# PEER layer on one Trainium2 core: the gelu-times-gate product moved between engines, and scores issued one query visit earlier

## The chip, the cores and the metric

The kernel runs on one core of a Trainium2 chip. The metric is the device time of one execution in microseconds; the lower the better. Three runs of the kernel before gave 4600.65, 4601.71 and 4601.87 us.

## What is computed

One layer of an encoder, in float32, for 1024 prompt tokens and 256 sample tokens of width 1024, with shared weights: two attentions, gated and merged, and then the expert retrieval that this change is about, followed by a norm:

```python
def peer(h, w_query, sub_keys, expert_u, expert_v):      # per chunk of 128 tokens
    qry = einsum('cd,dq->cq', xc, w_query).reshape(128, 8, 2, 128)
    sc = einsum('chpd,hpnd->chpn', qry, sub_keys)          # 8 heads, 2 halves, 128 keys
    s_top, i_top = top_k(sc, 16)
    cand = s_top[:, :, 0, :, None] + s_top[:, :, 1, None, :]
    best_s, pos = top_k(cand, 16)                          # 16 of 128*128 experts a head
    g = softmax(best_s)
    act = gelu(einsum('chkd,cd->chk', expert_u[idx], xc))
    return einsum('chk,chkd->cd', g * act, expert_v[idx])
```

So each token has 128 chosen experts, each with a gate g. The weight of an expert is g times gelu of a dot product.

## The kernel before, in words

The attentions and the whole sample part come first and are the same in both kernels. The change lies in the last phase, `phase_mixed` (L1663), over the eight tiles of 128 prompt tokens. Five of them (0 to 4, GATHERED) gather the rows of their experts; for three (5 to 7, DENSE) all 16384 experts are computed and multiplied by a dense table of gates.

**Order.** Every engine has its own program. All of them are written by the same walk, `Turns.walk` (L1571), which calls named pieces of work in one order; each engine does its share of a piece and skips those in which it has none. An engine does its work strictly in that order and waits on semaphores for the others.

**Queries.** The first loop of the walk has 39 visits v (L1574). Visit v issues query v (32 of them: TensorE, 16 matmuls, L2270) and, on ScalarE, the copy of query v-1 (L1949). Two queries make the 2 x 128 key scores of a head for four tiles. At odd visits from 3 on TensorE computes the scores (L2284); at the visit behind that ScalarE copies them out of PSUM (L1959) and stores them to DRAM, from where SP loads them, one head of one tile at a time (L1802). From visit 6 on VectorE picks (`choose`, L2090): the top 16 of each half, of the candidates, and decodes them to indices; the gates are made by `soften` and `gates` (L2143).

**Steps.** A step (n, g) works on pair g of the 128 chosen experts of gathered tile n; there are 64 + 1 for each tile. GpSimd gathers the rows u and v of an expert for 128 tokens in one indirect DMA (L1921) into a ring of 8 slots, that is 4 pairs, and may overwrite a pair when TensorE has `used` it. In step (n, g):
- VectorE (L2174) waits for gelu of pair g-1, multiplies ge by the gates g2 of that pair (L2178), and then computes the two dot products of pair g (L2186).
- ScalarE (L2009) waits for the dots of pair g and applies gelu to them (L2013); then it waits for the weights of pair g-1 and spreads each over a small diagonal matrix (L2020, two instructions).
- TensorE (L2309) waits for the diagonals of pair g-1 and multiplies the v rows by them (L2320, 32 small matmuls).

So everything of pair g-1 behind the gelu is done one step later than its dots. Steps are put between other work by `advance` (L1534): from visit 13 on one or two at a visit, by `1 + v % 2`, then among the building of the dense gates, then in the dense stage in proportion to planned costs (L1653).

**Dense tiles.** After the picks, VectorE, ScalarE and TensorE build one-hot matrices and the gates (L2170, L1993, L1995, L2305); ScalarE copies them (L2002) and stores them to DRAM, 2 MB at a time, from two buffers (L2006). Then the dense stage: 128 stage1 units (L2340, gelu on ScalarE at L2044) and 192 stage2 units (L2356, added on VectorE at L2221), with the other 237 steps between them.

Of the kernel before, what the change touches and what calls it, by code (L numbers as in the profile page):

```python
# [9 lines left out]
ALU = mybir.AluOpType  # L10
# [21 lines left out]
HEADS, KEYS, TOPK = 8, 128, 16  # L32
# [1492 lines left out]
class Turns:  # L1525
# [45 lines left out]
    def walk(self):  # L1571
        on, first, every = self.on, DENSE[0], slice(0, HEADS)
        ends = {0: 0, 1: 1, 3: 2, 5: 4, 7: 6}
        for v in range(39):  # L1574
            if v < 32:
# [3 lines left out]
            if v == 1:  # L1579
                on("late")  # L1580
            if v % 2 and 3 <= v <= 33:
                on("scores", (v - 3) // 2)
            if v % 2 == 0 and 4 <= v <= 34:
                on("spread_s", (v - 4) // 2)
            h, at = divmod(v - 6, 4)
            if 0 <= h < HEADS and at == 0:
# [8 lines left out]
            if h >= 0 and at == 3 and h < HEADS:  # L1595
                self.pick_dense(first + 1, h)
            if v >= 13:
                self.advance(1 + v % 2)
# [64 lines left out]
def phase_mixed(nc, tag, x2, g_ffn, w_query, sub_keys, experts, u_turned, g_final, ident_d, iota_d, fold_d, unfold_d,  # L1663
# [7 lines left out]
    with ExitStack() as ctx:  # L1671
# [65 lines left out]
        h_ld, row_ld = [m.sem(f"h_ld{b}") for b in range(2)], [m.sem(f"row_ld{r}") for r in range(RING)]  # L1737
        dotted, gelued, weighted, diag_ready, used = (m.sem(n) for n in ("dotted", "gelued", "weighted", "diag_ready", "used"))
        xr_ld, parts_ready, unfolded, y_ready, root2 = (m.sem(n) for n in ("xr_ld", "parts_ready", "unfolded", "y_ready", "root2"))
# [10 lines left out]
        order = []  # L1750
        Turns(lambda what, *a: order.append(a[:2]) if what == "choose" and a[2] == 0 else None).walk()

        def walk(**do):
# [33 lines left out]
        with nc.Block() as block:  # L1787
# [138 lines left out]
            def _(act):  # L1926
# [82 lines left out]
                def step(n, g):  # L2009
                    if g < STEPS:  # L2010
                        act.wait_ge(dotted, SLOTS * n + PAIR * (g + 1))
                        c = slice(PAIR * g, PAIR * (g + 1))
                        nc.scalar.activation(ge[:, c], dot[:, c], ACT.Gelu).then_inc(gelued, 1)  # L2013
                    if g >= 1:
                        act.wait_ge(weighted, STEPS * n + g)
                        if STEPS * n + g > 2:
                            act.wait_ge(used, STEPS * n + g - 2)
                        for c in range(PAIR):
                            s = PAIR * (g - 1) + c
                            last = nc.scalar.activation(diag[:, (g - 1) % 2, c, :], fold[:], ACT.Copy, scale=wgt[:, s:s + 1])  # L2020
                        last.then_inc(diag_ready, 1)
                    if n and g == 2:
                        norm_y(n)
# [41 lines left out]
            def _(dve):  # L2065
# [77 lines left out]
                def gates(tile, hs):  # L2143
                    nonlocal gated
                    gated += 1
                    to = gd_of(tile - DENSE[0]) if tile in DENSE else g2[:, tile % 2, :]
                    dve.wait_ge(exp_ready, gated)
                    link(nc.vector.reduce_sum(ssum[:, hs], soft_of(tile)[:, hs, :], AXX))
                    link(nc.vector.reciprocal(ssum[:, hs], ssum[:, hs]))
                    link(nc.vector.tensor_tensor(to.rearrange("p (h c) -> p h c", c=TOPK)[:, hs, :], soft_of(tile)[:, hs, :],  # L2150
                                                 ssum[:, hs].unsqueeze(2).to_broadcast([P, hs.stop - hs.start, TOPK]), ALU.mult))

                def turn(d):
# [20 lines left out]
                def step(n, g):  # L2174
                    if g >= 1:
                        dve.wait_ge(gelued, STEPS * n + g)
                        c = slice(PAIR * (g - 1), PAIR * g)
                        nc.vector.tensor_tensor(wgt[:, c], ge[:, c], g2[:, n % 2, c], ALU.mult).then_inc(weighted, 1)  # L2178
                    if g == 0 and n:
# [310 lines left out]
```

## Time and profile before

| | us |
|---|---|
| median of 3 runs | 4601.71 |
| the profiled execution | 4601.26 |
| its span, from first to last instruction | 4599.5 |
| the last phase starts its queries at | 2098 |
| first VectorE pick | 2138.4 |
| first unit of the dense stage that runs without a hole | 2901 |

The profile is of one execution. Engines: PE is TensorE, PEld its weight loads, DVE VectorE, ACT ScalarE, POOL GpSimd, SP the queue of SyncE. An L number is a line of the kernel.

### The profile page before, as it was taken

The page shows a single profiled execution, that of the slowest core. Times are in us where ns is not written, and L with a number is a line of the kernel's source. Part 1 is how long each engine was busy: PE and PEld are TensorE (multiplying, and loading weights), DVE is VectorE, ACT ScalarE, POOL GpSimd, SP SyncE. Part 2 cuts the span into 40 slices and gives each one's busy share as a digit, 9 for nine tenths or more (in the row PEclk, how much of TensorE's full clock was granted, in tenths as well). Part 3 has the DMA queues.
Part 4 walks back from the last instruction along what each step waited for, and adds up shares of the span by engine and source line. Part 5 has one row for each costly group of instructions (what it writes and reads, how often), then busy time and mean ns, then how long its engine had stood idle before and what let it go on. Part 6 is the DMA issues. An engine that isn't in the chain of part 4 may idle for free.

```text
span 4599.5 us, 61350 instructions
## 1 busy us (share of the span) xinstructions
PE 3988.8 (87%) x22629; PEld 2057.9 (45%) x22629; DVE 2836.5 (62%) x7114; ACT 1128.4 (25%) x2916; POOL 1254.2 (27%) x1018
## 2 busy tenths in 40 slices
PE   7786599998799989998983456799999999999998
PEld 3454444443577764444441334344444444444443
DVE  1332856775888876662778977455565556555544
ACT  0221111221455551112222565111111111111111
POOL 0200232221534513320232212233323323332332
PEclk9888799999899999998995688899999999999999
DMA  6243398896544348756688779999999999999997
GB/s 238 76 179 120 109 364 318 336 356 230 209 175 178 147 171 337 300 222 233 256 318 318 285 276 369 360 401 380 387 388 405 382 379 412 406 398 377 408 413 303
DMA packets 351290, 1370.42 MB, mean 298 GB/s; under 512 B 26896, under 2 KB 112528, under 8 KB 231568
## 3 DMA queue, kind: packets, MB, share of 16 engines
q0 software_dynamic: 129024, 939.58, 51.6%
q1 hardware_dynamic: 161840, 389.17, 22.6%
q10 hardware_dynamic: 60128, 37.75, 2.6%
q8 instruction: 180, 2.95, 0.3%
q14 instruction: 118, 0.97, 0.1%
HBM read 1277.22 MB, written 89.18 MB: 297 GB/s over the span
## 4 chain that ended last, share of the span: by engine, by line
PE 34%; DVE 10%; DMA 6%; issue 3%; ACT 2%; POOL 0%; SPq 0%; DVEq 0%; ACTq 0%; another core or an unknown queue 0%
PE prompt_exp_wk L2340 13%; PE prompt_exp_wk L2356 11%; PE prompt_exp_acc L2320 6%; DVE prompt_exp_junk L2186 4%; PE prompt_exp_wk L2270 4%; DMA prompt_exp_ring<-in_experts_dram,prompt_exp_idx 3%; DMA gates_dram<-prompt_exp_area 2%; DVE prompt_exp_hT L2170 1%; DVE prompt_exp_hit L2130 1%; DVE prompt_exp_topi L2081 1%; ACT prompt_exp_diag L2020 1%; PE prompt_exp_wk L2305 1%; DVE prompt_exp_top L2078 0%; DMA scores_dram<-prompt_exp_area 0%; PE prompt_exp_wk L2284 0%
## 5 line engine op out<-in xcount | busy, mean ns | idle before, releaser
L1921 POOL DMA_INDIRECT prompt_exp_ring<-in_experts_dram,prompt_exp_idx x640 | 698.6, 1092 | 1815.9 <-PE prompt_exp_acc L2320 1603.4
L2186 DVE CUSTOM_DVE_ANT_0 prompt_exp_junk<-prompt_exp_ring,prompt_exp_h 128x1024 bf16<-128x1024 f32 x640 | 765.2, 1223 | 167.6 <-DMA prompt_exp_ring<-in_experts_dram,prompt_exp_idx 166.9
L2340 PE MATMUL prompt_exp_wk<-prompt_exp_hT,prompt_exp_area 128*128 128x384 f32 x2048 | 697.5, 495 | 23.7 <-DMA prompt_exp_area<-in_u_turned_dram 23.7
L2356 PE MATMUL prompt_exp_wk<-prompt_exp_area 128*128 128x512 f32 x1536 | 702.8, 604 | 0.0
L537 PE MATMUL prompt_proj_acc<-normed_w,normed_hT 128*128 128x512 f32 x1280 | 553.7, 595 | 14.5 <-PEq L91 14.5
L2340 PEld LDWEIGHTS prompt_exp_wk<-prompt_exp_hT,prompt_exp_area 128*128 128x128 f32 x2048 | 385.8, 192 | 357.9 <-issue 97.6
L2320 PE MATMUL prompt_exp_acc<-prompt_exp_ring,prompt_exp_diag 32*32 32x512 f32 x10240 | 392.9, 643 | 173.5 <-ACT prompt_exp_diag L2020 170.3
L152 POOL DMA_INDIRECT sample_hid_ring<-in_experts_dram,sample_hid_idx x256 | 277.0, 1082 | 892.1 <-DVE sample_hid_acc L182 842.8
L2221 DVE TENSOR_TENSOR prompt_exp_area<-prompt_exp_area,prompt_exp_wk 128x512 f32<-128x512 f32 x186 | 127.8, 687 | 575.9 <-PE prompt_exp_wk L2356 543.4
L2356 PEld LDWEIGHTS prompt_exp_wk<-prompt_exp_area 128*128 128x128 f32 x1536 | 280.4, 190 | 425.8 <-issue 395.3
L537 PEld LDWEIGHTS prompt_proj_acc<-normed_w,normed_hT 128*128 128x128 f32 x1280 | 243.6, 191 | 318.4 <-issue 318.4
L165 DVE CUSTOM_DVE_ANT_0 sample_hid_junk<-sample_hid_ring,sample_hid_h 128x1024 bf16<-128x1024 f32 x256 | 349.9, 1367 | 44.2 <-DMA sample_hid_ring<-in_experts_dram,sample_hid_idx 33.8
L2013 ACT ACTIVATE prompt_exp_ge<-prompt_exp_dot 128x2 f32<-128x2 f32 x320 | 64.9, 203 | 1272.1 <-DVE prompt_exp_dot L2186 1265.8
L182 DVE SCALAR_TENSOR_TENSOR sample_hid_acc<-sample_hid_ring,sample_hid_w,sample_hid_acc 128x1024 f32<-128x1024 f32 x254 | 326.2, 1284 | 7.5
L2320 PEld LDWEIGHTS prompt_exp_acc<-prompt_exp_ring,prompt_exp_diag 32*32 32x32 f32 x10240 | 79.6, 106 | 375.9 <-ACT prompt_exp_diag L2020 253.4
L2305 PE MATMUL prompt_exp_wk<-prompt_exp_area,prompt_exp_hT 128*128 128x128 f32 x768 | 132.7, 342 | 112.9 <-DVE prompt_exp_hT L2170 76.4
L2305 PEld LDWEIGHTS prompt_exp_wk<-prompt_exp_area,prompt_exp_hT 128*128 128x128 f32 x768 | 122.3, 250 | 157.8 <-DVE prompt_exp_hT L2170 102.3
L2020 ACT ACTIVATE prompt_exp_diag<-prompt_exp_fold,prompt_exp_wgt 128x32 f32<-128x32 f32 x640 | 165.8, 306 | 11.6 <-DVE prompt_exp_wgt L2178 11.4
L2044 ACT ACTIVATE prompt_exp_area<-prompt_exp_wk 128x384 f32<-128x384 f32 x128 | 62.8, 490 | 358.4 <-PE prompt_exp_wk L2340 358.1
L537 PE MATMUL sample_proj_acc<-sample_proj_w,sample_proj_hT 128*128 128x512 f32 x320 | 140.5, 601 | 9.4 <-PEq L271 9.4
L998 PE MATMUL prompt_att_Op<-prompt_att_vB,prompt_att_pT_b 128*128 128x128 f32 x1024 | 125.9, 276 | 10.4 <-ACT prompt_att_pT_a L712 10.4
L174 DVE TENSOR_TENSOR sample_hid_w<-sample_hid_ge,sample_hid_g 128x1 f32<-128x1 f32 (+1 forms) x208 | 59.1, 284 | 115.0 <-ACT sample_hid_ge L203 114.8
(363 smaller groups left out, 5025.4 us busy)
## 6 DMA issues: line engine op xcount, KB each, us to landing
prompt_exp_area<-in_u_turned_dram SPq DMA_DIRECT2D x128, 512.0 KB
prompt_exp_area<-in_experts_dram SPq DMA_DIRECT2D x64, 1024.0 KB
gates_dram<-prompt_exp_area ACTq DMA_DIRECT2D x12, 2048.0 KB
prompt_exp_area<-gates_dram SPq DMA_DIRECT2D x32, 768.0 KB
sample_proj_w<-in_w_all_dram SPq DMA_DIRECT2D x10, 2048.0 KB, 20.0
normed_w<-in_w_all_dram SPq DMA_DIRECT2D x10, 2048.0 KB, 13.7
proj_dram<-prompt_proj_stage SPq DMA_DIRECT2D x80, 256.0 KB
prompt_exp_ring<-in_experts_dram,prompt_exp_idx POOLq DMA_INDIRECT x640
```

The costliest lines, as they stand in the source:

```text
L152: self.nc.gpsimd.indirect_dma_start(out=self.ring[:, s % self.RING, :], out_offset=None, in_=self.experts, in_offset=bass.IndirectOffsetOn ...
L165: self.nc.vector.tensor_tensor_reduce(out=self.junk[:], in0=self.ring[:, s % self.RING, 0:D], in1=self.h[:], scale=1.0, scalar=0.0, op0=AL ...
L182: nc.vector.scalar_tensor_tensor(self.acc[:], v, w, self.acc[:], ALU.mult, ALU.add).then_inc(self.added, 1)
L537: last = nc.tensor.matmul(acc[:, u % 4, :], hT[:, k, t * P:(t + 1) * P], w[:, c % NL, k, :], start=(k == 0), stop=(k == KD - 1))
L1921: nc.gpsimd.indirect_dma_start(out=ring[:, s % RING, :], out_offset=None, in_=experts, in_offset=bass.IndirectOffsetOnAxis(ap=idx[:, n % 2 ...
L2020: last = nc.scalar.activation(diag[:, (g - 1) % 2, c, :], fold[:], ACT.Copy, scale=wgt[:, s:s + 1])
L2186: nc.vector.tensor_tensor_reduce(out=junk[:, s % 2, :], in0=ring[:, s % RING, 0:D], in1=h2[:, n % 2, :], scale=1.0, scalar=0.0, op0=ALU.mu ...
L2270: last = nc.tensor.matmul(wk[:, v % 2, :], wq[:, h // 2 % 2, k, at:at + P], (hT1 if grp else hT0)[:, k, :], start=(k == 0), stop=(k == KD ...
L2305: last = nc.tensor.matmul(wk[:, 2 + i % 2, c * KEYS:(c + 1) * KEYS], onehot_a[:, i % 2 * BLOCK + c, :], onehot_b[:, i % 2, c, :], start=Tr ...
L2320: last = nc.tensor.matmul(acc[at:at + Q, part, :], diag[k, (g - 1) % 2, c, :], ring[k, s % RING, D + half * 512:D + half * 512 + 512], sta ...
L2340: last = nc.tensor.matmul(wk[:, j % 2, 0:TURNED], ut[:, j % 3, k, :], hT_dense[:, k, :], start=(k == 0), stop=(k == KD - 1))
L2356: last = nc.tensor.matmul(wk[:, 2 + o % 2, :], act_e[:, c % 2, j, t * P:(t + 1) * P], vt[:, half, j, :], start=(j == 0), stop=(j == JB - 1))
```

## The change

Two things. First, the loop of visits has 38 instead of 39; scores are computed at even visits from 2 on, in the order of the walk right behind the query of that visit, and all that follows them (copies and stores of scores, picks, gates, the steps from visit 12) moves one visit earlier. Second, the product of gelu and gate leaves VectorE: ScalarE makes it in its own part of the step, one instruction of one column for each of the two experts of the pair (a copy with the gate as its scale), between gelu of pair g and the diagonals of pair g-1. ScalarE waits for the gates by a new semaphore, once for each head, and for gelu of the pair; VectorE no longer waits for gelu, and before it writes gates over those of two tiles back it waits for that tile's last diagonals.

```diff
--- before.py
+++ after.py
@@ -1571,18 +1571,18 @@
     def walk(self):
         on, first, every = self.on, DENSE[0], slice(0, HEADS)
         ends = {0: 0, 1: 1, 3: 2, 5: 4, 7: 6}
-        for v in range(39):
+        for v in range(38):
             if v < 32:
                 on("query", v)
             if 1 <= v <= 32:
                 on("spread_q", v - 1)
             if v == 1:
                 on("late")
+            if v % 2 == 0 and 2 <= v <= 32:
+                on("scores", (v - 2) // 2)
             if v % 2 and 3 <= v <= 33:
-                on("scores", (v - 3) // 2)
-            if v % 2 == 0 and 4 <= v <= 34:
-                on("spread_s", (v - 4) // 2)
-            h, at = divmod(v - 6, 4)
+                on("spread_s", (v - 3) // 2)
+            h, at = divmod(v - 5, 4)
             if 0 <= h < HEADS and at == 0:
                 self.pick(GATHERED[0], h)
                 if h in ends:
@@ -1594,7 +1594,7 @@
                 self.pick_dense(first, h)
             if h >= 0 and at == 3 and h < HEADS:
                 self.pick_dense(first + 1, h)
-            if v >= 13:
+            if v >= 12:
                 self.advance(1 + v % 2)
         done = 0
 
@@ -1735,7 +1735,7 @@
         ij_ready, ij_turned, ij_spread = (m.sem(n) for n in ("ij_ready", "ij_turned", "ij_spread"))
         a_ready, b_ready, gp_full, gp_spread = (m.sem(n) for n in ("a_ready", "b_ready", "gp_full", "gp_spread"))
         h_ld, row_ld = [m.sem(f"h_ld{b}") for b in range(2)], [m.sem(f"row_ld{r}") for r in range(RING)]
-        dotted, gelued, weighted, diag_ready, used = (m.sem(n) for n in ("dotted", "gelued", "weighted", "diag_ready", "used"))
+        gates_ready, dotted, gelued, weighted, diag_ready, used = (m.sem(n) for n in ("gates_ready", "dotted", "gelued", "weighted", "diag_ready", "used"))
         xr_ld, parts_ready, unfolded, y_ready, root2 = (m.sem(n) for n in ("xr_ld", "parts_ready", "unfolded", "y_ready", "root2"))
         yo_ready, out_stored = m.sem("yo_ready"), m.sem("out_stored")
         u_ld, v_ld, gc_ld = [m.sem(f"u_ld{b}") for b in range(3)], [m.sem(f"v_ld{b}") for b in range(2)], [m.sem(f"gc_ld{b}") for b in range(2)]
@@ -1749,6 +1749,12 @@
 
         order = []
         Turns(lambda what, *a: order.append(a[:2]) if what == "choose" and a[2] == 0 else None).walk()
+
+        gate_order = []
+        Turns(lambda what, *a: gate_order.extend([a] if what == "gates" and a[0] in GATHERED else [])).walk()
+
+        def gates_upto(tile, h):
+            return 1 + next(i for i, (t, hs) in enumerate(gate_order) if t == tile and hs.start <= h < hs.stop)
 
         def walk(**do):
             Turns(lambda what, *a: do.get(what, idle)(*a)).walk()
@@ -2012,11 +2018,18 @@
                         c = slice(PAIR * g, PAIR * (g + 1))
                         nc.scalar.activation(ge[:, c], dot[:, c], ACT.Gelu).then_inc(gelued, 1)
                     if g >= 1:
+                        pair = slice(PAIR * (g - 1), PAIR * g)
+                        if pair.start % TOPK == 0:
+                            act.wait_ge(gates_ready, gates_upto(n, pair.start // TOPK))
+                        act.wait_ge(gelued, STEPS * n + g)
+                        for s in range(pair.start, pair.stop):
+                            last = nc.scalar.activation(wgt[:, s:s + 1], ge[:, s:s + 1], ACT.Copy, scale=g2[:, n % 2, s:s + 1])
+                        last.then_inc(weighted, 1)
                         act.wait_ge(weighted, STEPS * n + g)
                         if STEPS * n + g > 2:
                             act.wait_ge(used, STEPS * n + g - 2)
-                        for c in range(PAIR):
-                            s = PAIR * (g - 1) + c
+                        for s in range(pair.start, pair.stop):
+                            c = s % PAIR
                             last = nc.scalar.activation(diag[:, (g - 1) % 2, c, :], fold[:], ACT.Copy, scale=wgt[:, s:s + 1])
                         last.then_inc(diag_ready, 1)
                     if n and g == 2:
@@ -2144,11 +2157,15 @@
                     nonlocal gated
                     gated += 1
                     to = gd_of(tile - DENSE[0]) if tile in DENSE else g2[:, tile % 2, :]
+                    if tile in GATHERED and tile >= 2 and hs.start == 0:
+                        dve.wait_ge(diag_ready, STEPS * (tile - 1))
                     dve.wait_ge(exp_ready, gated)
                     link(nc.vector.reduce_sum(ssum[:, hs], soft_of(tile)[:, hs, :], AXX))
                     link(nc.vector.reciprocal(ssum[:, hs], ssum[:, hs]))
                     link(nc.vector.tensor_tensor(to.rearrange("p (h c) -> p h c", c=TOPK)[:, hs, :], soft_of(tile)[:, hs, :],
                                                  ssum[:, hs].unsqueeze(2).to_broadcast([P, hs.stop - hs.start, TOPK]), ALU.mult))
+                    if tile in GATHERED:
+                        dve.sem_inc(gates_ready, 1)
 
                 def turn(d):
                     dve.sem_inc(ij_ready, 1)
@@ -2172,10 +2189,6 @@
                     last.then_inc(a_ready, 1)
 
                 def step(n, g):
-                    if g >= 1:
-                        dve.wait_ge(gelued, STEPS * n + g)
-                        c = slice(PAIR * (g - 1), PAIR * g)
-                        nc.vector.tensor_tensor(wgt[:, c], ge[:, c], g2[:, n % 2, c], ALU.mult).then_inc(weighted, 1)
                     if g == 0 and n:
                         dve.wait_ge(h_ld[n % 2], 16 * ((n + 1) // 2))
                     if g < STEPS:
```

## Rows read from the trace of the kernel before

**Rows 1.** The profile page: span, and the busy time of each engine.
```profile
span 4599.5 us, 61350 instructions
PE 3988.8 (87%) x22629; PEld 2057.9 (45%) x22629; DVE 2836.5 (62%) x7114; ACT 1128.4 (25%) x2916; POOL 1254.2 (27%) x1018
```

**Rows 2.** Busy time by stage of the last phase: start:end, length, engines, clock, DMA share, GB/s.
```profile
2098.00:2200.00 102.00, 100.56 (x313) 51.29 (x314) 38.33 (x198) 22.16 (x38) 7.49 (x8) 0.99 0.51 194
2200.00:2434.00 234.00, 201.46 (x1480) 90.60 (x1478) 178.75 (x664) 50.83 (x144) 64.48 (x61) 0.92 0.82 313
2434.00:2650.00 216.00, 92.58 (x979) 55.05 (x979) 199.07 (x725) 92.24 (x262) 47.73 (x48) 0.61 0.76 285
2650.00:2855.00 205.00, 116.33 (x1343) 81.20 (x1344) 164.41 (x508) 122.48 (x322) 50.01 (x50) 0.83 0.89 324
2855.00:2901.00 46.00, 20.17 (x153) 10.31 (x152) 13.40 (x46) 5.04 (x17) 7.91 (x7) 0.80 1.01 380
2901.00:4584.00 1683.00, 1631.13 (x11200) 714.88 (x11200) 931.30 (x2196) 244.60 (x875) 520.98 (x468) 0.99 0.98 389
```

**Rows 3.** Chain of waits, in order of time: start, length, what.
```profile
2134.39 13.74 PE prompt_exp_wk L2270 x32
2148.13 1.78 PE prompt_exp_wk L2284 x16
...
2668.61 26.37 DMA gates_dram<-prompt_exp_area
...
3513.60 3.65 PE prompt_exp_wk L2356 x8
```

**Rows 4.** Waits of TensorE, 2901 to 4600: us in total, times, longest.
```profile
PE prompt_exp_acc L2320 <- ACT prompt_exp_diag L2020: 43.8, 49, 6.7
PE prompt_exp_wk L2340 <- DMA prompt_exp_area<-in_u_turned_dram: 23.7, 1, 23.7
```

**Rows 5.** Timeline of one step in the dense stage: start, length, engine, line.
```profile
3517.27 0.69 DVE L2221 TENSOR_TENSOR prompt_exp_area<-prompt_exp_area,prompt_exp_wk 128x512 f32<-128x512 f32 x1 [6.13 <-PE prompt_exp_wk L2356]
...
3517.88 0.15 DVE L2178 TENSOR_TENSOR prompt_exp_wgt<-prompt_exp_ge,prompt_exp_g 128x2 f32<-128x2 f32 x1
3517.95 1.22 DVE L2186 CUSTOM_DVE_ANT_0 prompt_exp_junk<-prompt_exp_ring,prompt_exp_h 128x1024 bf16<-128x1024 f32 x1
...
3520.36 0.20 ACT L2013 ACTIVATE prompt_exp_ge<-prompt_exp_dot 128x2 f32<-128x2 f32 x1 [7.29 <-DVE prompt_exp_dot L2186]
3520.47 0.52 ACT L2020 ACTIVATE prompt_exp_diag<-prompt_exp_fold,prompt_exp_wgt 128x32 f32<-128x32 f32 x2
...
3521.03 1.15 PE L2320 MATMUL prompt_exp_acc<-prompt_exp_ring,prompt_exp_diag 32*32 32x512 f32 x32 [0.37 <-ACT prompt_exp_diag L2020]
```

**Rows 6.** Timeline of the next step, whose diagonals are just in time.
```profile
3526.82 0.52 ACT L2020 ACTIVATE prompt_exp_diag<-prompt_exp_fold,prompt_exp_wgt 128x32 f32<-128x32 f32 x2
3527.48 1.14 PE L2320 MATMUL prompt_exp_acc<-prompt_exp_ring,prompt_exp_diag 32*32 32x512 f32 x32
```

**Rows 7.** ScalarE's square root of one column with an operand from memory: ns min/median/max.
```profile
L1933 ACT ACTIVATE prompt_exp_stat<-prompt_exp_stat,prompt_exp_eps x8: 294/294/297, 2083.1 to 2101.7; 128x1 f32<-128x1 f32 x8
```

**Rows 8.** Timeline, building of the gates: absolute values, relu, blocks.
```profile
2706.04 1.26 ACT L1993 ACTIVATE prompt_exp_area<-prompt_exp_iota,prompt_exp_ijgT 128x128 f32<-128x128 f32 x4
...
2707.33 0.63 ACT L1995 ACTIVATE prompt_exp_area<-prompt_exp_area 128x512 f32<-128x512 f32 x1
...
2708.06 2.02 PE L2305 MATMUL prompt_exp_wk<-prompt_exp_area,prompt_exp_hT 128*128 128x128 f32 x16 [0.72 <-issue]
```

**Rows 9.** Waits in 2200 to 2434 (first) and 2650 to 2855 (the others).
```profile
DVE prompt_exp_wgt L2178 <- ACT prompt_exp_ge L2013: 7.9, 14, 2.8
...
DVE prompt_exp_wgt L2178 <- ACT prompt_exp_ge L2013: 6.0, 3, 4.5
...
PE prompt_exp_acc L2320 <- ACT prompt_exp_diag L2020: 38.8, 19, 8.7
```

**Rows 10.** Timeline: VectorE's first pick of the last phase.
```profile
2138.38 0.49 DVE L2078 MAX8 prompt_exp_top<-prompt_exp_scl 128x8 f32<-128x128 f32 x2 [34.35 <-DMA prompt_exp_scl<-scores_dram]
```

## The prediction

> **What bounds the kernel now.** The page comes first: one core, a span of 4599.5 us in a profiled execution of 4601.26, with TensorE busy 87% and ScalarE 25% [rows 1]. That share says ScalarE has room; it does not say whether anybody waits for it. So the second view is the busy time by stage [rows 2], over the last phase alone, the only one that the change touches. The first 2098 us keep their time. Then come: queries alone (to about 2200), queries with picks and the first steps (to 2434), the tail of the picks (to 2650, VectorE busy 199 of 216 us), the building of the dense gates (to 2855), a hole while the last gates are stored (to 2901), and the dense stage of 1683 us, with TensorE busy 97% of it and the DMA engines 98%.
>
> The third view, the chain of waits, says who sets the end of each [rows 3]. Early it runs through the queries: a pair of them takes 13.7 us, with 1.8 of scores behind it. In the building it runs twice through a store of gates (the first 26 us), with stretches of TensorE, VectorE and ScalarE between. In the dense stage it is TensorE's own matmuls, one behind the other. So in that stage, each time TensorE stands idle is paid in full, and the fourth view lists these: 49 times, 43.8 us together, TensorE waits for the diagonals of ScalarE [rows 4].
>
> **What such a wait is made of** [rows 5]. Two stage2 units stand back to back. VectorE adds the first (3517.27), multiplies the weights of the last pair (3517.88), makes two dot products (3517.95 to 3520.33); ScalarE does gelu (3520.36), then two diagonals (3520.47 to 3520.99); TensorE starts at 3521.03, 0.37 us late. The diagonals belong to the pair before and have all they need, but ScalarE is an in-order engine and takes them behind the gelu that waits for the new dots. Most of the waits have exactly this 0.37; nine are over 1 us, most of them where a gathered row came late. Where a stage1 unit (5.4 us) or another step stands in between, there is slack: of the 237 steps of the stage, read one by one, four of those that don't wait have under 0.5 us (the tightest that one sees 0.10 [rows 6]), some 30 have 0.6 to 1.0 and the rest more.
>
> **Part 1: the product moves to ScalarE.** VectorE loses one instruction per step, 0.155 us long, but the dot behind it starts 0.07 us after it, so 0.07 is what a busy VectorE gains in the dense stage [rows 5]. It loses the wait for gelu as well. ScalarE gains per step two products of 128x1 whose scale is read from memory, and a wait for its own result, ahead of the diagonals. No row shows this product. Nearest is the square root of 128x1 with an operand from memory, 0.294 [rows 7]; two diagonals overlap so that the second starts 0.21 behind the first [rows 5]; an engine that waits for its own result resumes 0.03 behind it [rows 8]. That is 0.21 + 0.29 + 0.03 = 0.53. Bounds: from below two operations as cheap as gelu, which lets the next one start after 0.11 and lasts 0.20 [rows 5]: 0.34; from above two diagonals of 0.31 that don't overlap, with two waits: 0.68. I take 0.5, since the square root is nearest in size and kind and a column fewer than the diagonal's 32 helps the overlap. Less VectorE's 0.07: the diagonals are ready 0.43 later (0.27 to 0.61).
> The Trainium skill speaks against this half (ScalarE: Activation LUTs, Rules for kernel authors): a plain multiplication belongs on VectorE. By that rule alone the half is a loss wherever ScalarE is waited for; without it the sum below would be the 7 us of part 2 and the kernel would come to 4594. The trace agrees as far as it goes: one instruction of 0.155 us does both columns on VectorE, in the rows above.
>
> Dense stage: 49 x 0.43 = **+21 us** (13 to 30). The four tight ones add under 1, and the ones at 0.6 and more are not reached. What the delay hides in: where a row came late TensorE waits 1.2 to 6.7 us, and as rows are requested behind earlier steps, a slower TensorE gives them some of that back: I take **-3** (0 to -10).
>
> Building of the gates: here TensorE waits 19 times for diagonals, 38.8 us [rows 9]. ScalarE is in the loop: behind the diagonals it makes four absolute values and a relu, and TensorE's blocks start 0.10 us after that relu ends [rows 8]; VectorE's next block waits for them. So 0.43 per step goes into the loop, but not where ScalarE then waits for a store anyway. 14 of the 24 steps: **+6** (0 to +10). The 6.0 us that VectorE waits for gelu [rows 9] give nothing: 4.5 of them come while ScalarE sits behind a store of gates, and its diagonals come no sooner.
>
> Where VectorE is the bound (some 30 steps between 2254 and 2650): 0.1 us each for the instruction, and part of the 7.9 us of waits for gelu before 2434 [rows 9], which fall between the two steps of an odd visit: **-4** (-1 to -10).
>
> The new waits: for the gates of a tile, and of the gates for the diagonals of two tiles back. Both are satisfied long before. The first is signalled by VectorE ahead of the dots for which ScalarE has just waited; the second comes at step 55 of the tile before, over 50 steps after the diagonals it asks for. The third, for gelu, is of the operation one step back. Queued behind them are gelu of the dense units and the blocks, priced above. Nothing is cast for them: cover gone, they would cost a step.
>
> **Part 2: scores one visit earlier.** Scores, their copies, stores and loads (ScalarE's and SP's queues), picks, gates and steps all keep their places to each other; only the queries move one visit back. VectorE's first pick waits 34.35 us for scores [rows 10], behind four queries; now behind three, so 6.9 us sooner. PE, the copies and the banks allow it: the second query's copy ends during the third query. The steps start one query sooner and the tail has one visit fewer; the number of steps before the dense stage stays 39 + 49. Whether queries or VectorE set the pace in between, one query's time is gone: **-7 us** (0, if late scores or rows fill the gap, to -10, a visit's length once steps run in it).
>
> **Sum.** -7 - 4 + 6 + 21 - 3 = +13. On the profiled 4601.3 this gives **4614 us**; the median of the runs, 4601.7, is 0.4 more and changes nothing.
>
> **Rivals.**
> (a) The dense stage is paced by DMA, not TensorE: its engines are 98% taken at 389 GB/s [rows 2]. Then the added waits vanish in the rows' landing and the sum is -7 - 4 + 6 = -5: 4596, no change. For it: the share. Against: TensorE's idle time in the stage comes from the diagonals, and of its waits for data only one, at the start, is for a DMA of weights [rows 4]. 0.22.
> (b) Faster: VectorE, freed of its wait for gelu, runs ahead where it is the bound. It takes hold if over half of the 14 waits before 2434 and of the slots there lie on the chain, and the building's stores swallow ScalarE's part: -10 - 10 + 0, and the dense stage gives at most +5 through (a): 4586. For it: VectorE's 199 of 216 us. Against: in the dense stage TensorE's waits were seen. 0.15.
> (c) ScalarE's products don't overlap: 0.61 net, 49 x 0.61 = 30, building +10, no relief: 4629. 0.10.
> (d) The scores part brings nothing, as VectorE finds its scores or rows late after all: 4621. 0.08.
> My forecast (4605 to 4622) has 0.45.
>
> **The numbers.** A measurement of this kernel can tell 0.2%, 9.2 us, from no change: under 4592.5 is faster, over 4610.9 slower. Faster: (b) and an edge of (a), 0.18. Same: the rest of (a), and the forecast's lower edge, where the product is as cheap as its lower bound, 0.31. Slower 0.51. The range from 4590 to 4628 leaves out most of (b) and half of (c). The forecast's own is 4605 to 4622.
>
> **What would show it.** The new products near 0.29 us, the diagonals starting some 0.6 us behind gelu in place of 0.11. In the dense stage the typical wait goes from 0.37 to 0.8, and TensorE's waits for diagonals from 43.8 us to about 65; the stage from 1683 to about 1700. VectorE's first pick 6.9 us earlier, at 2131.5; the dense stage starting within 5 us of before. I am wrong if the waits grow and the stage doesn't (a), if the start of the dense stage comes 15 us or more sooner (b), or if the product costs under 0.2.

## The result, and the profile after

Over 20 runs of each, before has a median of 4601.48 us and the changed kernel one of 4612.24: a ratio of 1.0022, 95% interval 1.0016 to 1.0029. That is 10.8 us slower by the medians: clear of no change, and about the 0.2% that a measurement here can tell. Two executions of before took 6192.01 and 14898.58 us; they are left out of the ratio. The profiled execution of the changed kernel took 4617.22, 5 us above its median, while that of before (4601.26) stands at its median.

The page's head, against [rows 1]: ScalarE has 640 instructions and 151 us more, VectorE 320 instructions and 36 us less, TensorE the same number of matmuls.

```profile
span 4615.4 us, 61687 instructions
...
PE 3997.3 (87%) x22629; PEld 2063.3 (45%) x22629; DVE 2800.2 (61%) x6794; ACT 1279.5 (28%) x3556; POOL 1241.1 (27%) x1018
```

The same stages as [rows 2], each cut where the changed kernel reaches the same point (start:end, length, PE, PEld, DVE, ACT, POOL, clock, DMA share, GB/s):

```profile
2098.00:2200.00 102.00, 100.58 (x314) 51.01 (x313) 46.55 (x240) 22.28 (x37) 7.51 (x8) 0.99 0.51 191
2200.00:2434.00 234.00, 201.39 (x1510) 89.51 (x1508) 177.15 (x626) 67.73 (x214) 67.14 (x64) 0.92 0.86 330
2434.00:2638.00 204.00, 91.79 (x979) 55.75 (x979) 186.25 (x671) 101.71 (x303) 42.98 (x44) 0.60 0.76 281
2638.00:2850.00 212.00, 128.65 (x1345) 90.27 (x1314) 162.13 (x479) 132.72 (x367) 55.13 (x49) 0.77 0.88 317
2850.00:2895.66 45.66, 19.84 (x151) 10.05 (x149) 12.19 (x41) 6.79 (x25) 6.78 (x8) 0.74 0.97 370
2895.66:4615.40 1719.74, 1633.98 (x11216) 714.27 (x11216) 916.00 (x1970) 364.11 (x1362) 506.49 (x468) 0.99 0.97 382
```

The last line counts the stage to its end; before it is

```profile
2901.06:4599.50 1698.44, 1634.31 (x11216) 715.39 (x11216) 940.55 (x2207) 252.64 (x888) 520.98 (x468) 0.99 0.97 387
```

So TensorE is busy for the same 1634 us in a stage that is 21.3 us longer: all of the difference is idle time. The wait that carries it, in place of the 43.8 us of [rows 4] (columns as there):

```profile
PE prompt_exp_acc L2333 <- ACT prompt_exp_diag L2033: 65.1, 54, 6.6
```

and one such wait, the same step as in [rows 5]:

```profile
3516.48 0.69 DVE L2234 TENSOR_TENSOR prompt_exp_area<-prompt_exp_area,prompt_exp_wk 128x512 f32<-128x512 f32 x1 [6.05 <-PE prompt_exp_wk L2369]
...
3517.08 1.22 DVE L2199 CUSTOM_DVE_ANT_0 prompt_exp_junk<-prompt_exp_ring,prompt_exp_h 128x1024 bf16<-128x1024 f32 x1
...
3519.49 0.20 ACT L2019 ACTIVATE prompt_exp_ge<-prompt_exp_dot 128x2 f32<-128x2 f32 x1 [7.51 <-DVE prompt_exp_dot L2199]
3519.60 0.47 ACT L2026 ACTIVATE prompt_exp_wgt<-prompt_exp_ge,prompt_exp_g 128x1 f32<-128x1 f32 x2
3520.10 0.53 ACT L2033 ACTIVATE prompt_exp_diag<-prompt_exp_fold,prompt_exp_wgt 128x32 f32<-128x32 f32 x2
...
3520.68 1.15 PE L2333 MATMUL prompt_exp_acc<-prompt_exp_ring,prompt_exp_diag 32*32 32x512 f32 x32 [0.81 <-ACT prompt_exp_diag L2033]
```

VectorE's add to the first dot is 0.60 us where it was 0.68. Gelu to the first diagonal is 0.61 where it was 0.11. The wait is 0.81 where it was 0.37: 0.44 more. The product by itself (ns least/median/most), the square root's 0.294 of [rows 7] beside it:

```profile
L2026 ACT ACTIVATE prompt_exp_wgt<-prompt_exp_ge,prompt_exp_g x640: 277/279/297, 2205.7 to 4588.7; 128x1 f32<-128x1 f32 x160
```

The first pick, against [rows 10]:

```profile
2130.79 0.49 DVE L2091 MAX8 prompt_exp_top<-prompt_exp_scl 128x8 f32<-128x128 f32 x2 [28.07 <-DMA prompt_exp_scl<-scores_dram]
```

Its place relative to the first query, 34.2 us in place of 40.4, is the fairer reading, since the phase starts 1.4 us sooner in this execution. Cut into three lengths, queries and picks / building to the start of the dense stage / dense stage: before 399.6 / 403.5 / 1698.4 us, after 389.0 / 410.0 / 1719.7. (Building starts where ScalarE first copies the turned picks, at 2497.6 and 2485.6.) The dense stage thus starts 5.4 us sooner than in before.

Each such length is of one execution. Two kernels were profiled twice (e3 and e10, e7 and e11 below), and their lengths differ by 2.2 and 3.0 us in the first stretch, 0.2 and 0.7 in the second, 2.4 and 0.6 in the third. Differences of that size say nothing here. The spans of before and after differ by 15.9 us, the medians by 10.8.

### The profile page after: what moved, and what is told of

It reads as the page before. It is cut to its first block, busy times and chain, and to the rows that moved or that the text cites. A ratio compares the mean times of both kernels' runs of the same rounds, so it can differ in the third digit from the quotient of the medians.

```text
span 4615.4 us, 61687 instructions
## 1 busy us (share of the span) xinstructions
PE 3997.3 (87%) x22629; PEld 2063.3 (45%) x22629; DVE 2800.2 (61%) x6794; ACT 1279.5 (28%) x3556; POOL 1241.1 (27%) x1018
## 3 DMA queue, kind: packets, MB, share of 16 engines
q8 instruction: 180, 2.95, 0.3%
## 4 chain that ended last, share of the span: by engine, by line
PE 32%; DVE 10%; DMA 7%; issue 3%; ACT 2%; POOL 1%; SPq 0%; DVEq 0%; ACTq 0%; POOLq 0%
PE prompt_exp_wk L2353 12%; PE prompt_exp_wk L2369 10%; PE prompt_exp_acc L2333 6%; DMA prompt_exp_ring<-in_experts_dram,prompt_exp_idx 4%; DVE prompt_exp_junk L2199 4%; PE prompt_exp_wk L2283 3%; DMA gates_dram<-prompt_exp_area 2%; DVE prompt_exp_hT L2187 1%; PE prompt_exp_wk L2318 1%; DVE prompt_exp_topi L2094 1%; DVE prompt_exp_hit L2143 1%; ACT prompt_exp_diag L2033 1%; POOL prompt_exp_ring L1927 1%; ACT prompt_exp_wgt L2026 1%; DVE prompt_exp_top L2091 0%
## 5 line engine op out<-in xcount | busy, mean ns | idle before, releaser
L1927 POOL DMA_INDIRECT prompt_exp_ring<-in_experts_dram,prompt_exp_idx x640 | 686.0, 1072 | 1844.9 <-PE prompt_exp_acc L2333 1641.2
L2318 PE MATMUL prompt_exp_wk<-prompt_exp_area,prompt_exp_hT 128*128 128x128 f32 x768 | 142.9, 361 | 103.5 <-DVE prompt_exp_hT L2187 76.8
L2318 PEld LDWEIGHTS prompt_exp_wk<-prompt_exp_area,prompt_exp_hT 128*128 128x128 f32 x768 | 132.0, 267 | 149.5 <-DVE prompt_exp_hT L2187 112.9
L2026 ACT ACTIVATE prompt_exp_wgt<-prompt_exp_ge,prompt_exp_g 128x1 f32<-128x1 f32 x640 | 148.9, 280 | 0.0
## 6 DMA issues: line engine op xcount, KB each, us to landing
prompt_exp_area<-gates_dram SPq DMA_DIRECT2D x32, 768.0 KB, 13.5
```

Of the source, the lines that this page charges most:

```text
L1927: nc.gpsimd.indirect_dma_start(out=ring[:, s % RING, :], out_offset=None, in_=experts, in_offset=bass.IndirectOffsetOnAxis(ap=idx[:, n % 2 ...
L2026: last = nc.scalar.activation(wgt[:, s:s + 1], ge[:, s:s + 1], ACT.Copy, scale=g2[:, n % 2, s:s + 1])
L2318: last = nc.tensor.matmul(wk[:, 2 + i % 2, c * KEYS:(c + 1) * KEYS], onehot_a[:, i % 2 * BLOCK + c, :], onehot_b[:, i % 2, c, :], start=Tr ...
```

## The experiments

Eleven kernels, in three groups that each shared their runs of before: e1 to e4 (4599.36 us), e5 to e8 (4601.93) and e9 to e11 (4599.11). Ratios are to before of the same group.

### The two halves apart

e1 is the changed kernel with the old walk, so the product alone; e2 is before with the new walk, so the scores alone.

```diff
 # e1, in the changed kernel
-        for v in range(38):
+        for v in range(39):
...
-            if v % 2 == 0 and 2 <= v <= 32:
-                on("scores", (v - 2) // 2)
+            if v % 2 and 3 <= v <= 33:
+                on("scores", (v - 3) // 2)
 # e2: the same lines the other way round, in the kernel before
```

> The change's first half alone: product on ScalarE, scores at their old visits. Theory (ScalarE's two products lie on TensorE's path in the dense stage, and the two halves add): 4612 plus the 7 us of the second half, so 4619 us (4615 to 4624), 1.0035 to 1.005 of the kernel before; TensorE's waits for the diagonals in the dense stage about 65 us, as in the changed kernel; VectorE's first pick at 2138. Rival (the scores part brings nothing): 4612, no slower than the changed kernel.

> The change's second half alone: scores one visit earlier, product on VectorE. Theory: 7 us less than before, 4594 us (4590 to 4598), waits for the diagonals in the dense stage about 44 us as before, building of the gates starting about 8 us sooner. Rival (the earlier scores are hidden by late rows, and the 12 us by which the building starts sooner come from the product): 4601, building starting at its old time.

e1: 4622.09 us, 1.0052 (1.0038 to 1.0065). e2: 4587.45, 0.9969 (0.9956 to 0.9981). Both are clear of no change, on opposite sides: +22.7 and -11.9 us. Added they give the +10.8 that was measured. Scores alone gave more than expected. TensorE's waits in the dense stage follow the product and not the scores (e1, then e2):

```profile
PE prompt_exp_acc L2333 <- ACT prompt_exp_diag L2033: 64.6, 54, 6.6
```

```profile
PE prompt_exp_acc L2320 <- ACT prompt_exp_diag L2020: 45.4, 51, 6.7
```

By stage, e1 has 400.7 / 405.0 / 1719.1 and e2 385.8 / 404.3 / 1701.1 us. So the product costs 1.1, 1.5 and 20.7 us against before, and 3.2, 5.7 and 18.6 as the changed kernel against e2. The scores bring 13.8 us (e2 against before) and 11.7 (the changed kernel against e1) in the queries and picks; the later stretches are 3.5 and 5.6 us longer and give part of it back.

### Is it the product, or where it stands?

In each step ScalarE first waits for the new dots (gelu of pair g), then makes product and diagonals of pair g-1, which had all they need. e3 keeps all of the change and only puts the waiting part last. e4 does the same to the kernel before.

```diff
-                    if g < STEPS:
-                        act.wait_ge(dotted, SLOTS * n + PAIR * (g + 1))
-                        c = slice(PAIR * g, PAIR * (g + 1))
-                        nc.scalar.activation(ge[:, c], dot[:, c], ACT.Gelu).then_inc(gelued, 1)
                     if g >= 1:
...
                         last.then_inc(diag_ready, 1)
+                    if g < STEPS:
+                        act.wait_ge(dotted, SLOTS * n + PAIR * (g + 1))
+                        c = slice(PAIR * g, PAIR * (g + 1))
+                        nc.scalar.activation(ge[:, c], dot[:, c], ACT.Gelu).then_inc(gelued, 1)
```

> The changed kernel with ScalarE's order in a step turned round: products and diagonals of the pair before, which have all they need, and only then gelu, which waits for the new dots. Theory (the price is paid because the diagonals stand behind that gelu): waits of TensorE for diagonals in the dense stage fall from 65 us to under 27, the stage gets some 35 us shorter, and the time is about 4573 us (4566 to 4582). Rival (DMA paces the dense stage): the waits turn into waits for rows, and the time stays over 4595.

> The kernel before with the same order in ScalarE's step: diagonals before gelu, product still on VectorE at the head of its step. Theory: the dense stage's waits fall from 44 us to under 27, the building's by some us, the time by 20 to 25 us to about 4579 (4572 to 4587). Rival (DMA paces the stage): over 4595. If the product on ScalarE is harmless once it is off the path, this one is slower than the third of this call by the 7 us of the scores, and no more than that.

e3: 4530.19 us, 0.9849 (0.9835 to 0.9862). e4: 4549.1, 0.9893 (0.9878 to 0.9908). Both beat their expectation by far (4573 and 4579 were written down). TensorE's waits in the dense stage, e3 and then e4:

```profile
PE prompt_exp_acc L2333 <- ACT prompt_exp_diag L2029: 8.8, 3, 6.4
```

```profile
PE prompt_exp_acc L2320 <- ACT prompt_exp_diag L2016: 14.3, 5, 4.7
```

The typical short wait is gone, not shortened. In e3's timeline the diagonals don't wait for the next dots: they are ready at 3400.5, ScalarE then waits 5.24 us for dots, and TensorE uses them at 3405.97 without any wait:

```profile
3399.98 0.53 ACT L2029 ACTIVATE prompt_exp_diag<-prompt_exp_fold,prompt_exp_wgt 128x32 f32<-128x32 f32 x2
...
3405.75 0.20 ACT L2034 ACTIVATE prompt_exp_ge<-prompt_exp_dot 128x2 f32<-128x2 f32 x1 [5.24 <-DVE prompt_exp_dot L2199]
...
3405.97 1.14 PE L2333 MATMUL prompt_exp_acc<-prompt_exp_ring,prompt_exp_diag 32*32 32x512 f32 x32
```

More came than the 43.8 us of waits could explain, and the windows say from where (dense stage of e3, then of e4; columns as above):

```profile
2877.35:4528.80 1651.45, 1622.33 (x11216) 711.42 (x11216) 921.66 (x1970) 374.30 (x1362) 514.31 (x468) 0.99 0.99 398
```

```profile
2886.21:4545.00 1658.79, 1622.98 (x11216) 712.45 (x11216) 943.80 (x2207) 268.63 (x888) 528.10 (x468) 0.99 0.98 396
```

e4's stage is 39.6 us shorter than that of before. Of this, 29.5 is the wait for diagonals (43.8 to 14.3) and 11.3 is TensorE's own busy time (1634.31 to 1622.98), for the same number of matmuls. Ahead of the stage, queries and picks take 388.8 us in e4 and 371.6 in e3; building (404.8 and 407.5) gained nothing.

### Each microsecond in that place

e5 doubles the products: it makes each of them a second time, into a column that nobody reads.

```diff
-                        for s in range(pair.start, pair.stop):
-                            last = nc.scalar.activation(wgt[:, s:s + 1], ge[:, s:s + 1], ACT.Copy, scale=g2[:, n % 2, s:s + 1])
+                        for to, s in [(to, s) for to in (stat, wgt) for s in range(pair.start, pair.stop)]:
+                            last = nc.scalar.activation(to[:, s:s + 1] if to is wgt else stat[:, 0, 8 + s % PAIR:9 + s % PAIR],
+                                                        ge[:, s:s + 1], ACT.Copy, scale=g2[:, n % 2, s:s + 1])
```

> The changed kernel with each product made twice on ScalarE (the first pair goes to columns that nobody reads), so four products ahead of the diagonals. The trace of the changed kernel shows two products in 0.47 us, 0.19 apart, so this adds 0.38 us to each step. Theory: the dense stage's 54 waits grow by 0.38 each, some 20 us, and steps that had 0.1 to 0.4 us of slack join them: waits for diagonals from 65 to about 90 us, time 4612 + 25 = 4637 us (4630 to 4650). Rival (the 21 us of the dense stage come from VectorE's changed timing or from DMA, not from the length of ScalarE's work): within 5 us of 4612.

4629.81 us, 1.006 (1.0046 to 1.0074): slower than the changed kernel again, by 17.6 us, where 4637 was written down.

```profile
PE prompt_exp_acc L2333 <- ACT prompt_exp_diag L2033: 79.2, 53, 6.6
```

```profile
3529.91 1.15 PE L2333 MATMUL prompt_exp_acc<-prompt_exp_ring,prompt_exp_diag 32*32 32x512 f32 x32 [1.19 <-ACT prompt_exp_diag L2033]
```

The typical wait goes 0.37, 0.81, 1.19: by 0.4 with each pair of products. Sorted by size, the waits of up to 1.25 us are 42 of 17.6 us in before, 45 of 36.2 in the changed kernel and 45 of 49.4 here. So the typical wait grows by what stands ahead of it, each time, but the sum of the short ones by 18.6 and then by 13.2 us only. The longer waits stay about as they are (7 of 26.2 us, 9 of 28.9, 8 of 29.8). The dense stage is 7.8 us longer than in the changed kernel: 14.1 us more of waits, but 5.5 us less of busy time (the last section says where that comes from).

### Where in time, and which part must come first

e6 makes the product on ScalarE only up to the end of the building of the gates (step 16 of the second tile), and on VectorE, ahead of the dots, from then on. e7 is e2 with the order of e3: scores moved, product on VectorE, gelu last. e8 is the changed kernel with its two products alone ahead of the wait for the dots, while the diagonals stay behind gelu.

```diff
 # e6, VectorE's step
+                    if g >= 1 and late_pair(n, g):
+                        dve.wait_ge(gelued, STEPS * n + g)
...
+                        nc.vector.tensor_tensor(wgt[:, c], ge[:, c], g2[:, n % 2, c], ALU.mult).then_inc(late_weighted, 1)
 # e8, ScalarE's step: the products move up
+                    if g >= 1:
+                        act.wait_ge(gelued, STEPS * n + g)
...
+                        last.then_inc(weighted, 1)
                     if g < STEPS:
                         act.wait_ge(dotted, SLOTS * n + PAIR * (g + 1))
```

> The changed kernel with the product back on VectorE from step (1, 17) on, which is where the dense stage begins; before it ScalarE makes it. Theory: the dense stage is as long as before (1698 to 1701 us, waits for diagonals 44 us), what lies ahead of it is as in the changed kernel; time 4612 - 20 = 4591 us (4585 to 4597). If the product costs as much ahead of the dense stage as the two half changes suggest (their dense stages start at 2884 and 2896), it stays some 4 us above the kernel with the scores part alone, else level with it.

> Scores one visit earlier, product on VectorE, diagonals before gelu on ScalarE. It differs from the fastest so far (4530 us) only in who makes the product. Theory (with the diagonals first, neither gelu nor ScalarE's products are waited for by TensorE, and VectorE is nearer to being the bound): 4536 us (4530 to 4545), the product on ScalarE being worth 0 to 10 us. Rival (a plain product is dearer on ScalarE in any order): under 4528.

> The changed kernel with only the two products moved ahead of gelu in ScalarE's step; the diagonals stay behind gelu. ScalarE does exactly as much. Theory (what costs is the products' place, not their presence): the diagonals again start 0.11 us behind gelu, waits in the dense stage 41 to 46 us, time 4588 us less what VectorE gains, 4585 (4578 to 4592). Rival (any more work on ScalarE costs this): 4607 to 4617.

e6: 4590.46 us, 0.9976 (0.9967 to 0.9985). e7: 4539.39, 0.9859 (0.9842 to 0.9876). e8: 4583.85, 0.9958 (0.9944 to 0.9973).

e6 against e2 (0.9969, in another group; the intervals overlap): having ScalarE multiply while VectorE is the bound brings nothing that can be seen (queries and picks 385.6 us against e2's 385.8). In the building it costs 7.0 us (411.3 against 404.3). Its 45.5 us of waits in the dense stage are e2's 45.4. e8 says that the product costs nothing once nobody stands behind it. Its products and e2's are the same work on two engines, and e8 is not slower:

```profile
PE prompt_exp_acc L2334 <- ACT prompt_exp_diag L2034: 40.5, 48, 6.6
```

```profile
3515.67 0.20 ACT L2027 ACTIVATE prompt_exp_ge<-prompt_exp_dot 128x2 f32<-128x2 f32 x1 [6.86 <-DVE prompt_exp_dot L2200]
3515.78 0.52 ACT L2034 ACTIVATE prompt_exp_diag<-prompt_exp_fold,prompt_exp_wgt 128x32 f32<-128x32 f32 x2
...
3516.35 1.15 PE L2334 MATMUL prompt_exp_acc<-prompt_exp_ring,prompt_exp_diag 32*32 32x512 f32 x32 [0.29 <-ACT prompt_exp_diag L2034]
```

Gelu to diagonal is 0.11 again, and the wait 0.29 in place of before's 0.37, since VectorE has one instruction fewer ahead of its dots. That is the 0.08 for which the prediction took 0.07.

### With the order right, which engine should multiply?

e9 is e1 with gelu last (product on ScalarE, scores as before). e10 is e3 over again, e11 is e7 over again, all in one group.

```diff
 # e9 = e1 with the edit of e3; e10 = e3; e11 = e7
```

> The eighth corner of the two halves and the order: product on ScalarE, scores at their old visits, diagonals before gelu. Theory (the scores part is worth 7 to 14 us in any order): 4530 + 10 = 4540 us (4535 to 4547), 5 to 10 us below the kernel before with diagonals first. Rival (the scores part gives nothing once nobody waits for gelu): 4530.

> The fastest kernel again (changed kernel, diagonals before gelu), beside the next one on the same chip: 4530 us (4526 to 4535).

> Scores earlier, diagonals before gelu, product on VectorE, again. If the product on ScalarE is a gain once it is off TensorE's path, this is 5 to 10 us slower than the one before it in this call, with intervals that don't touch; if it is neither gain nor loss, within 3 us.

e9: 4541.22 us, 0.9871 (0.9856 to 0.9886). e10: 4532.63, 0.9851 (0.9837 to 0.9865). e11: 4539.17, 0.9865 (0.9849 to 0.988). The product on ScalarE is 8 to 9 us *faster* than on VectorE by the medians (e9 against e4, e3 against e7; 10 and 5 us by the ratios, since the groups' runs of before differ) and 6.5 faster in the one pair of the same group (e10 against e11). The sign is the same three times, but the intervals of e10 and e11 overlap, where I had expected them apart: likely, not shown. The scores part brings 8.6 us in this order (e10 against e9), about what it brings in the old one.

The waits say where a part of it lies. e4's five waits for diagonals in the dense stage (14.3 us) all stand behind `decode`, 8.3 us in which VectorE turns picks of a later tile into indices: the product on VectorE queues behind it, and the diagonals wait for the product.

```profile
3355.45 0.16 DVE L2178 TENSOR_TENSOR prompt_exp_wgt<-prompt_exp_ge,prompt_exp_g 128x2 f32<-128x2 f32 x1
...
3355.65 0.53 ACT L2016 ACTIVATE prompt_exp_diag<-prompt_exp_fold,prompt_exp_wgt 128x32 f32<-128x32 f32 x2 [5.99 <-DVE prompt_exp_wgt L2178]
```

With the product on ScalarE the waits are 8.8 us in e3, 9.5 in e10 and 10.3 in e9, against 14.3, 13.6 and 13.5 in e4, e7 and e11.

e3 is the best version that ran: 4530.19 and, again, 4532.63 us, a ratio of 0.985 to before both times.

## Why the prediction came out right, and which of its terms did not

Forecast and rivals: the slower side, the price and the place were as forecast (4614 against 4612.24). By its own steps:

- **Dense stage, +21.** Measured +21.3 in stage length, with the waits going 43.8 to 65.1, and +20.7 in e1. The delay per wait, 0.43, was 0.44 in the step quoted. Two products take 0.47 us and the first diagonal starts 0.50 behind the first of them, the value taken. The square root of [rows 7] (0.294) was the right neighbour of the product (0.279).
- **Relief of late rows, -3.** Not there, and its premise was a misreading. The prediction has nine waits over 1 us, "most of them where a gathered row came late". By the timeline of before it was so for two of the nine (2.00 us at 2984 and 1.75 at 3322). Two of 1.17 stand behind VectorE's multiplication of the dense gates (L2211, 1.76 us), and the other five, 22.5 us in all, behind `decode`. One of these (VectorE ends `decode` and does its dots at once; no row is late):

```profile
3151.54 0.22 DVE L2135 SCALAR_TENSOR_TENSOR prompt_exp_idx<-prompt_exp_part 128x64 int32<-128x64 f32 x1
3151.91 0.16 DVE L2178 TENSOR_TENSOR prompt_exp_wgt<-prompt_exp_ge,prompt_exp_g 128x2 f32<-128x2 f32 x1
3152.05 1.23 DVE L2186 CUSTOM_DVE_ANT_0 prompt_exp_junk<-prompt_exp_ring,prompt_exp_h 128x1024 bf16<-128x1024 f32 x1
...
3155.14 1.63 PE L2320 MATMUL prompt_exp_acc<-prompt_exp_ring,prompt_exp_diag 32*32 32x512 f32 x32 [4.86 <-ACT prompt_exp_diag L2020]
```

  A slower TensorE has no late row to relieve there, and the waits over 1.25 us went from 26.2 us to 28.9.
- **Building, +6.** Measured +6.5 here, +5.7 against e2, +7.0 in e6 against e2 and only +1.5 in e1. The size lies within what was allowed; why e1 stands apart is open.
- **VectorE where it is the bound, -4.** Not there. Queries and picks take 1.1 us more in e1 than in before, 3.2 more in the changed kernel than in e2 and 0.2 less in e6 than in e2, all about what two profiles of one kernel differ by. VectorE alone doesn't set the time there. In before's chain of waits from the last query (2407) to the building (2498), 39.8% is the gathering of rows, and GpSimd, which starts it, waits for TensorE to free a pair:

```profile
POOL prompt_exp_ring L1921 <- PE prompt_exp_acc L2320: 64.1, 11, 13.2
```

- **Scores, -7.** Right in mechanism, too small: 8.6 to 12 us in the medians. The first pick came 6.2 us sooner relative to the first query, as said. The queries themselves take about as long as before (from the first to the last 309.6 us in before, 308.3 in e1, 307.5 in the changed kernel, 304.8 in e2). The gain shows in the tail: from the last query to the building takes 90.0 us in before and 92.4 in e1, against 81.5 in the changed kernel and 81.1 in e2. The prediction had seen "the tail has one visit fewer" and then counted one query's time alone. Priced as a visit, its own bound of 10, the term would have been nearer.

The misses go opposite ways: 3 and 4 us taken as gained that were not, and 2 to 5 us of the scores' gain not counted. That the +13 lies so near the +10.8 of the medians is therefore partly luck; the profiled executions differ by 15.9. There was a miscount that did no harm: it gives 39 + 49 steps ahead of the dense stage, and the walk issues 41 ahead of the building and 40 in it.

The rivals. **(a)** that DMA paces the stage and swallows the waits is refuted by e1: +20.7 us in the stage, with the DMA share at 0.97. In e3 DMA comes nearer to it, with a share of 0.99 at 398 GB/s and VectorE waiting for rows 292 us in place of 117, but TensorE is still busy 1622 of the 1651 us:

```profile
DVE prompt_exp_junk L2199 <- DMA prompt_exp_ring<-in_experts_dram,prompt_exp_idx: 292.2, 182, 3.3
```

**(b)** that a freed VectorE wins outright is refuted by e1, which is slower, and e6, which is no faster than e2. **(c)** that the products don't overlap: no, 0.47 for two of 0.279, so the second starts 0.19 behind the first. **(d)** that the scores part brings nothing: no, e2.

The rule of the Trainium skill (ScalarE: Activation LUTs, Rules for kernel authors: a plain multiplication belongs on VectorE) came out as the trace had it in this order of work, at 22.7 us (e1). The lengths point the same way: 0.155 us for both columns on VectorE, 0.47 for the two on ScalarE. With the order of e3 the kernel was no slower for breaking it. The rule prices the instruction; what decided was what stood in the queue behind it, and ahead of it.

What the prediction did not ask is the larger thing. It had described the queue exactly (the diagonals "have all they need, but ScalarE is an in-order engine and takes them behind the gelu that waits for the new dots") and took it as given. Turning it round is worth 50 us in the kernel before (e4) and 82 in the changed one (e3), against the 23 us that the product cost.

## What to carry to other kernels

In an engine that works in order, what is issued behind a wait, or behind long work, inherits it. Before pricing an instruction that moves onto it, list what stands ready behind each wait, and put that ahead first; here the same two products cost 23 us behind the wait and nothing, or less, ahead of it. A saved instruction on a busy engine is worth time only where a profile by stage shows that engine setting the end. Before calling a wait that of a late transfer, look at what the engine at its head did just before: here it was mostly busy with other work. When a schedule loses a whole step of a loop, price the step's time in the tail too, and not only at its head.

## What the runs showed of the chip that I had not expected

**TensorE's matmuls can slow down behind a long wait.** In before, TensorE waits 1.75 us for diagonals until 3321.69, and the stage1 unit behind it takes 7.12 us where the one before took 5.32:

```profile
3305.22 5.32 PE L2340 MATMUL prompt_exp_wk<-prompt_exp_hT,prompt_exp_area 128*128 128x384 f32 x16
...
3321.69 1.15 PE L2320 MATMUL prompt_exp_acc<-prompt_exp_ring,prompt_exp_diag 32*32 32x512 f32 x32 [1.75 <-ACT prompt_exp_diag L2020]
...
3322.78 7.12 PE L2340 MATMUL prompt_exp_wk<-prompt_exp_hT,prompt_exp_area 128*128 128x384 f32 x16
```

The windows give the granted clock (the first of the last three values): 1.00 over the 20 us before, 0.91 over the next 20, and 0.50 in the middle of the slow unit, which is the lower of the clock's two levels, 1.2 in place of 2.4 GHz:

```profile
3300.00:3320.00 20.00, 19.95 (x138) 8.05 (x136) 10.14 (x28) 1.74 (x7) 6.04 (x6) 1.00 1.02 418
3320.00:3340.00 20.00, 17.94 (x130) 7.84 (x131) 9.48 (x18) 2.38 (x10) 3.91 (x5) 0.91 1.02 416
3324.00:3326.00 2.00, 2.00 (x4) 1.01 (x3) 0.03 (x2) 0.00 (x0) 1.70 (x2) 0.50 1.03 414
```

A wait can thus cost more than its own length, but not each one does. Behind its first unit, before's dense stage has eleven waits of TensorE over 1.2 us. Eight have a stretch at the lower clock beside them, and three have none (2.11 us at 3228, 2.95 at 3847, 3.10 at 4068). The window behind the second of these:

```profile
3840.00:3860.00 20.00, 17.05 (x117) 7.45 (x102) 11.38 (x25) 4.57 (x10) 6.33 (x6) 1.00 1.01 418
```

In the clock records of the traces the dense stage stands at the lower level for 46.4 us in before and 27.2 in e4, 50.7 in the changed kernel and 38.0 in e5. Taking half of that time as lost is an estimate, and it gives 9.6 us for before against e4, of 11.3 us of busy time, and 6.4 for the changed kernel against e5, where 5.5 were measured. Why e5's long waits met the lower clock less often (four of the twelve over 1.3 us) is open. The typical waits of 0.37, and of 0.81 in the changed kernel, did not cost anything of this kind: busy time is 1634 us with both.

Left open: the larger gain of e3 and e7 ahead of the dense stage (371.6 us for queries and picks in e3, against 389.0 in the changed kernel). Diagonals that are ready sooner let TensorE free its pair, and GpSimd gather the next one, sooner; that fits the chain in the tail, which e3 passes in 71.5 us in place of 81.5, but it was not tried by itself. Open too is the part of the product's gain on ScalarE in the new order that the 4 to 5 us of waits don't cover.
